# Rounded operands and rests in stick-breaking scores and values, and the HGRN2 output's last k tiles as two units

## The chip, the cores and the metric

The kernel runs on one core of a Trainium2 chip. The metric is the time of one execution on the device in microseconds; the median of several runs is compared. One profiled execution gives the trace.

## What is computed

A two-layer block (FoX attention, conv FFN, HGRN2, conv FFN) is followed by a hybrid block (retention and stick-breaking attention side by side, merged by gates, then SwiGLU). There are 512 tokens and 16 meta tokens, a width of 1024, all in fp32. The parts that the change touches are, in short:

```python
# HGRN2 mixer, after the heads
o = rms_norm(o, o_gain).reshape(B, L, D) * sigmoid(g)
h = h + o @ w_out
h = h + conv_ffn(h, ...)

# stick-breaking, 16 heads of 64
z = einsum('bhtd,bhsd->bhts', q, k) * scale
valid = (s_pos < t_pos) & (s_pos >= PAD)
log_not = where(valid, log_sigmoid(-z), 0)
after = cumsum(log_not, reverse over s) - log_not
a = where(valid, exp(log_sigmoid(z) + after), 0)
y = einsum('bhts,bhse->bhte', a, v)
```

## The kernel before

Everything is held transposed, features on the 128 partitions and the 528 tokens along them, so a width of 1024 is 8 tiles (`KT`). Weight products are made of rounded operands and rests: `wh`, `xh` are the fp32 values rounded to the type fp32r, `wl`, `xl` are what is left, and three fp32r matmuls (`wh` by `xh`, `wh` by `xl`, `wl` by `xh`) stand for one fp32 product. Such a product covers 528 tokens as two matmuls of 264 columns (L445), or 512 tokens as one (L441, a "narrow" group).

A *unit* is the weights for one output tile, up to 8 k tiles of 128x128. SyncE loads units into 4 slots of `raw` (`sp_unit`); ScalarE makes `wh` (`act_hi`, L404), VectorE makes `wl` (`dve_lo`, L408), each into 2 slots, one unit ahead of TensorE (`split_ahead`). A *group* is the accumulation of one output tile in PSUM (`pe_group`). Every engine runs its own list in order, and semaphores tie the lists together: `w_split`, `mm_done`, `psum_free`. `Phase` holds the numbers of units and groups of a stage, and the order of work on each engine is written out by hand.

**HGRN2 output.** The first 6 of 8 k tiles of the output product (`HG_EARLY`) are done during the last head. The last 2 k tiles are the phase `PH_HGOUT`: 8 groups, one for each output tile, of 12 matmuls each, each with a unit of its own (2 k tiles, 128 KB). For each tile VectorE adds the group to `h` (L516), ScalarE makes the gained copy `xh` (L463) and a square (L471), VectorE makes the rest `xl` (L475), and GpSimd adds the squares up (L486). Then the up-projection `PH_UP1` of the FFN follows.

**Stick-breaking.** The heads go two by two, with the loop of `sb_pair` on each engine. For a head TensorE makes the scores in PSUM from `s_k` and `s_q` (`sb_z`, L1034, fp32, 64 partitions), adds a mask (L1038), and after softplus it subtracts sums over later keys in fp32r (`sb_sums`, L1045, from the rounded `s_sh` and the rest `s_sl`). ScalarE turns the result into weights `s_a`, and `sb_values` (L1066, fp32) multiplies them by the transposed values `s_vt`; each head writes its own 64 partitions of PSUM bank 3. Softplus is Abs, Exp and Ln on ScalarE (L1540, L1543, L1546), a max-and-add on VectorE (L2249), a rounded copy on ScalarE and a rest on VectorE (L2253). Each of these works in three pieces, of 512, 400 and 432 columns.

Between these parts TensorE makes the four projections of the next pair (`ahead_`), in the order value, gate, query, key:

```python
            ahead_(0)
            if not isinstance(i, int) or i:
                sb_values(i - 1, 1)
            sb_sums(2 * i)
            ahead_(1)
            pe.wait_ge(s("sb_a"), 2 * i + 1)
            sb_z(1)
            ahead_(2)
            ...
            sb_values(i, 0)
            sb_sums(2 * i + 1)
            ahead_(3)
            ...
                sb_z(0)
```

`sb_turn` transposes the values of the next pair ahead of the last `sb_z(0)`.

## Time and profile before

| | |
|---|---|
| Median of 3 runs | 2936.13 us (2931.22 to 2941.09) |
| Profiled execution, its own time | 2934.11 us |
| Its span | 2932.4 us |
| TensorE (PE) busy | 2839.7 us, 97% |
| VectorE (DVE), ScalarE (ACT), GpSimd (POOL) busy | 1501.4, 1120.2, 210.7 us |
| Mean granted clock of TensorE | 0.985 |

PE is TensorE's matmuls, PEld its weight loads. Times in rows are microseconds from the start of the span. A fp32 matmul shows as two records in the trace, an fp32r matmul as one. Busy times of matmuls that follow each other overlap, so the time from start to start tells what one costs. A granted clock of 1.00 is 2.4 GHz, 0.50 is 1.2 GHz. An arrow `<-` names what ended the idle time before an instruction.

### The profile page before, as it was taken

The numbers are of one execution on the slowest core, as the hardware profiler recorded it, in microseconds if no ns is written. First come the engines' busy times: TensorE is split into PE (matmuls) and PEld (weight loads), VectorE is DVE, ScalarE is ACT, GpSimd is POOL, SyncE is SP. The second block draws the span as 40 slices with busy tenths as digits, with TensorE's granted clock in tenths as the row PEclk, the third lists the DMA queues.
The fourth block names the chain that finished last, engine by engine and source line by source line (L and its number), as shares of the span: only waits on it lengthen the run. The fifth ranks groups of instructions, "written<-read, shape, count | busy, mean of one in ns | idle before, by whom it ended". The sixth has DMA issues, their size and how long they took to land.

```text
span 2932.4 us, 46554 instructions
## 1 busy us (share of the span) xinstructions
PE 2839.7 (97%) x17851; PEld 2501.2 (85%) x17851; DVE 1501.4 (51%) x2168; ACT 1120.2 (38%) x1795; POOL 210.7 (7%) x177
## 2 busy tenths in 40 slices
PE   7999899999989999799999999999999999799998
PEld 7889799999989999799888888787888778588886
DVE  6767755553367775555533355364433335544422
ACT  4444443332245553433322223223344453422232
POOL 1000010000122220100001001001000000200000
PEclk9999999999999999899999999999999999899999
DMA  4222122323321111233233232332211112233322
GB/s 122 63 72 72 44 87 86 93 85 93 88 88 54 50 49 39 85 93 93 83 99 102 71 97 64 89 89 58 81 49 50 50 43 87 64 93 94 96 87 75
DMA packets 419559, 225.63 MB, mean 77 GB/s; under 512 B 7589, under 2 KB 416422, under 8 KB 419350
## 3 DMA queue, kind: packets, MB, share of 16 engines
q1 hardware_dynamic: 416438, 211.45, 24.9%
q0 software_dynamic: 2256, 10.32, 1.1%
q10 hardware_dynamic: 784, 2.75, 0.3%
q8 instruction: 55, 0.90, 0.1%
q14 instruction: 26, 0.21, 0.0%
HBM read 222.36 MB, written 2.13 MB: 77 GB/s over the span
## 4 chain that ended last, share of the span: by engine, by line
PE 63%; DVE 5%; issue 2%; ACT 1%; POOL 0%; DVEq 0%; ACTq 0%; POOLq 0%
PE ps L441 34%; PE ps L445 17%; PE ps L1045 2%; PE ps L861 2%; PE ps L1003 1%; PE ps L1066 1%; PE ps L1034 1%; PE ps L970 1%; DVE wl L408 1%; PE ps L906 1%; PE ps L1038 0%; DVE h L526 0%; DVE rl L2188 0%; DVE xl L475 0%; PE ps L895 0%
## 5 line engine op out<-in xcount | busy, mean ns | idle before, releaser
L408 DVE TENSOR_TENSOR wl<-raw,wh 128x1024 fp32r<-128x1024 f32 (+4 forms) x429 | 518.5, 1209 | 400.5 <-ACT wh L404 397.0
L404 ACT ACTIVATE wh<-raw 128x1024 fp32r<-128x1024 f32 (+4 forms) x429 | 428.4, 999 | 729.2 <-PE ps L441 395.1
L445 PE MATMUL ps<-xh,wh 128*128 128x264 f32 x2736 | 569.7, 289 | 13.4 <-DVE xl L475 6.0
L445 PE MATMUL ps<-xl,wh 128*128 128x264 f32 x2736 | 557.9, 285 | 0.0
L445 PE MATMUL ps<-xh,wl 128*128 128x264 f32 x2736 | 557.5, 285 | 0.0
L445 PEld LDWEIGHTS ps<-xh,wh 128*128 128x128 f32 x2736 | 428.4, 189 | 24.1 <-issue 6.1
L445 PEld LDWEIGHTS ps<-xl,wh 128*128 128x128 f32 x2736 | 425.6, 189 | 0.0
L445 PEld LDWEIGHTS ps<-xh,wl 128*128 128x128 f32 x2736 | 424.4, 189 | 0.0
L441 PE MATMUL ps<-xh,wh 128*128 128x512 f32 x976 | 392.2, 402 | 17.9 <-DVE xl L475 14.1
L441 PE MATMUL ps<-xl,wh 128*128 128x512 f32 x976 | 388.5, 398 | 0.0
L441 PE MATMUL ps<-xh,wl 128*128 128x512 f32 x976 | 386.1, 396 | 0.0
L441 PEld LDWEIGHTS ps<-xh,wh 128*128 128x128 f32 x976 | 184.5, 189 | 67.1 <-DVE xl L475 13.4
L441 PEld LDWEIGHTS ps<-xh,wl 128*128 128x128 f32 x976 | 185.2, 190 | 42.2
L441 PEld LDWEIGHTS ps<-xl,wh 128*128 128x128 f32 x976 | 184.7, 189 | 41.4 <-issue 1.4
L441 PE MATMUL ps<-hidh,wh 128*128 128x512 f32 x352 | 138.8, 394 | 0.4 <-DVE wl L408 0.4
L441 PE MATMUL ps<-hidh,wl 128*128 128x512 f32 x352 | 138.9, 395 | 0.0
L441 PE MATMUL ps<-hidl,wh 128*128 128x512 f32 x352 | 138.1, 392 | 0.0
L1729 DVE TENSOR_TENSOR pre<-ps,rstd 128x528 f32<-128x528 f32 (+1 forms) x66 | 46.4, 702 | 168.7 <-PE ps L445 110.4
L1729 DVE TENSOR_TENSOR t<-ps,rstd 128x512 f32<-128x512 f32 (+1 forms) x66 | 46.0, 697 | 145.7 <-PE ps L441 103.9
L486 POOL TENSOR_TENSOR ssq<-ssq,sq 128x528 f32<-128x528 f32 (+1 forms) x56 | 81.9, 1462 | 394.8 <-ACT sq L471 290.2
L1729 DVE TENSOR_TENSOR rt<-ps,rstd 128x512 f32<-128x512 f32 (+1 forms) x53 | 36.9, 697 | 141.7 <-PE ps L441 101.9
L488 POOL COPY ssq<-sq 128x528 f32<-128x528 f32 (+1 forms) x8 | 6.6, 826 | 1389.2 <-ACT sq L471 1130.5
(319 smaller groups left out, 4039.5 us busy)
## 6 DMA issues: line engine op xcount, KB each, us to landing
raw<-in_w_in SPq DMA_DIRECT2D x88, 512.0 KB, 4.0
raw<-in_ffn_w_gate SPq DMA_DIRECT2D x44, 512.0 KB, 3.8
raw<-in_ffn_w_up SPq DMA_DIRECT2D x44, 512.0 KB, 3.9
raw<-in_w_ffn_in SPq DMA_DIRECT2D x44, 512.0 KB, 3.8
raw<-in_fox_w_in SPq DMA_DIRECT2D x33, 512.0 KB, 4.1
raw<-in_hgrn_w_in SPq DMA_DIRECT2D x32, 512.0 KB, 4.0
raw<-in_ffn_w_down SPq DMA_DIRECT2D x32, 448.0 KB, 3.4
raw<-in_ffn_w_down SPq DMA_DIRECT2D x16, 512.0 KB, 3.6
```

Of the source, the lines that this page charges most:

```text
L404: nc.scalar.activation(wh[:, v % 2, 0:nk, :], raw[:, v % RAW_SLOTS, 0:nk, :], ACT.Copy).then_inc(s("w_hi"), 1)
L408: nc.vector.tensor_tensor(wl[:, v % 2, 0:nk, :], raw[:, v % RAW_SLOTS, 0:nk, :], wh[:, v % 2, 0:nk, :].bitcast(F32), ALU.subtract).then_in ...
L441: last = nc.tensor.matmul(ps[:, bank, 0:SEQ], w[:, slot, kk, :], x[:, k0 + k, META:L], start=first, stop=end_)
L445: last = nc.tensor.matmul(ps[:, bank + b, 0:HALF], w[:, slot, kk, :], x[:, k0 + k, b * HALF:(b + 1) * HALF], start=first, stop=end_)
L486: nc.gpsimd.tensor_tensor(ssq[:, t0:L], ssq[:, t0:L], sq[:, m % 2, t0:L], ALU.add).then_inc(s("sq_used"), 1)
L861: last = nc.tensor.matmul(ps[:, 2 + k % 2, P * c:P * (c + 1)], left[:, P * c:P * (c + 1)], right[:, P * c:P * (c + 1)], start=True, stop=True)
L906: last = nc.tensor.matmul(flat[:, at:at + TOK[j]], g_left[:, j * (j - 1) // 2 + c, :], g_f[:, P * j:P * j + TOK[j]], start=True, stop=True)
L970: last = nc.tensor.matmul(flat[0:TOK[j], at:at + SEQ - QFIRST[j]], rt[:, 2 + c, P * j:P * j + TOK[j]], rt[:, c, META + QFIRST[j]:L], start ...
L1003: last = nc.tensor.matmul(ps[:, 4 + e, QFIRST[j]:SEQ], r_vt[0:k, j, P * e:P * (e + 1)], r_s[0:k, QSTRIP[j]:QSTRIP[j] + SEQ - QFIRST[j]], s ...
L1034: nc.tensor.matmul(flat[:, QSTRIP[j]:QSTRIP[j] + SEQ - QFIRST[j]], s_k[lo:hi, P * j:P * j + P], s_q[lo:hi, QFIRST[j]:SEQ], start=(j < 3), ...
L1045: return nc.tensor.matmul(dst, w[:, :], src, start=False, stop=last, skip_group_check=True)
L1729: return V.tensor_tensor(shown(ph, gj, dst), out_of(ph, gj), shown(ph, gj, rstd[:, :]), ALU.mult)\
```

## The change

In stick-breaking, keys and queries are rounded (`sb_hi`, ScalarE) and their rests made (`sb_lo`, VectorE). `s_kp` holds for each head of the pair the rounded keys on its own 64 partitions and the rests on the other 64; `s_qh` and `s_ql` hold the rounded queries and their rests on both halves. A head's scores are two fp32r matmuls per key tile. The attention weights and the values are split the same way (`s_sh`, `s_sl`, `s_vh`, `s_vl`), and the values product is three fp32r matmuls per key tile. In `s_vh` and `s_vl` a block of zeros lies between the two heads' values, and both heads accumulate in all 128 partitions of bank 3. The order of the projections becomes key, query, value, gate. The buffers `s_sp`, `s_a` and `s_vt` go; their work moves to `s_e`, `s_sh` and `s_sl`. The outputs and gates lose their 16 meta columns.

At the HGRN2 output the last two k tiles become two units, each holding all 8 output tiles of one k tile (512 KB, rows that lie together), which are split before the last head's norm. TensorE still works output tile by output tile. ScalarE's squares run three tiles behind its copies, and VectorE's rests one tile behind its adds.

```diff
@@ phases
-PH_HGOUT = Phase(PH_HGL, 2, [[KT - HG_EARLY]] * 4, (0, 2) if ... else (2, 0))
+PH_HGOUT = Phase(PH_HGL, 1, [[KT]] * (KT - HG_EARLY), (0, 2) if ... else (2, 0))
+PH_HGOUT.gpi = KT
-PH_SB = Phase(PH_SBP, FOX_H // 2 - 1, K8, SB_BANKS, narrow=(1, 2))
+PH_SB = Phase(PH_SBP, FOX_H // 2 - 1, K8, SB_BANKS, narrow=(1, 3))
@@ SyncE: units of weights
+        for uj in range(PH_HGOUT.upi):
+            k = HG_EARLY + uj
+            sp_unit(sp, PH_HGOUT, 0, uj, dram["hgrn_w_out"][0][P * k:P * (k + 1), :].rearrange("p (m n) -> p m n", n=P))
...
-            sp_unit(sp, PH_SB, i, 0, sb_v(i, P))
-            sp_unit(sp, PH_SB, i, 1, gate_b(i, 0))
-            sp_unit(sp, PH_SB, i, 2, sb_q(i, P))
-            sp_unit(sp, PH_SB, i, 3, sb_k(i, P))
+            sp_unit(sp, PH_SB, i, 0, sb_k(i, P))
+            sp_unit(sp, PH_SB, i, 1, sb_q(i, P))
+            sp_unit(sp, PH_SB, i, 2, sb_v(i, P))
+            sp_unit(sp, PH_SB, i, 3, gate_b(i, 0))
@@ TensorE: HGRN2 output
+        for m in range(KT):
+            bank = PH_HGOUT.banks[(PH_HGOUT.g0 + m) % 2]
+            pe.wait_ge(s("psum_free"), PH_HGOUT.g0 + m + 1)
+            for uj in range(PH_HGOUT.upi):
+                k, slot = HG_EARLY + uj, (PH_HGOUT.u0 + uj) % 2
+                if m == 0:
+                    pe.wait_ge(s("w_split"), unit(PH_HGOUT, 0, uj) + RAW_SLOTS + 1)
+                    pe.wait_ge(s("y_ready"), KT + k + 1)
+                for n, (w, y) in enumerate(((wh, yh), (wh, yl), (wl, yh))):
+                    for b in range(2):
+                        last = nc.tensor.matmul(ps[:, bank + b, 0:HALF], w[:, slot, m, :], y[:, k, b * HALF:(b + 1) * HALF],
+                                                start=(uj + n == 0), stop=(uj + 1 == PH_HGOUT.upi and n == 2))
+                if m == KT - 1:
+                    last.then_inc(s("mm_done"), 1)
+            if m < KT - 1:
+                last.then_inc(s("late_mm"), 1)
@@ TensorE: scores and values
-                nc.tensor.matmul(flat[:, QSTRIP[j]:QSTRIP[j] + SEQ - QFIRST[j]], s_k[lo:hi, P * j:P * j + P],
-                                 s_q[lo:hi, QFIRST[j]:SEQ], start=(j < 3), stop=False, skip_group_check=True)
+                for n, q in enumerate((s_qh[:, b, :], s_ql[b][:, :])):
+                    nc.tensor.matmul(flat[:, QSTRIP[j]:QSTRIP[j] + SEQ - QFIRST[j]], s_kp[:, b, P * j:P * j + P],
+                                     q[:, QFIRST[j]:SEQ], start=(j < 3 and n == 0), stop=False, skip_group_check=True)
...
+            for ready, a, vs in (("sb_sh", s_sh, (s_vh, s_vl)), ("sb_sl", s_sl, (s_vh,))):
+                pe.wait_ge(s(ready), 6 * (2 * i + b) + 6)
+                for j in range(NTT):
+                    for v in vs:
+                        last = nc.tensor.matmul(ps[:, 3, QFIRST[j]:SEQ], v[:, j, b:b + 2, :].rearrange("p b n -> p (b n)"),
+                                                a[:, QSTRIP[j]:QSTRIP[j] + SEQ - QFIRST[j]], ...)
@@ TensorE: a pair
-            ahead_(0)
             if not isinstance(i, int) or i:
                 sb_values(i - 1, 1)
+            ahead_(0)
             sb_sums(2 * i)
             ahead_(1)
-            pe.wait_ge(s("sb_a"), 2 * i + 1)
+            pe.wait_ge(s("sb_a"), 6 * i + 3)
+            pe.wait_ge(s("sb_lo"), 2 * i + 2)
             sb_z(1)
-            ahead_(2)
-            pe.wait_ge(s("sb_vt_ready"), i + 1)
+            pe.wait_ge(s("sb_vt_lo"), i + 1)
             pe.wait_ge(s("sb_o_done"), i + 1)
             sb_values(i, 0)
+            ahead_(2)
             sb_sums(2 * i + 1)
             ahead_(3)
             if not last:
-                pe.wait_ge(s("psum_free"), evacuated(PH_SB, i, 0))
+                pe.wait_ge(s("psum_free"), evacuated(PH_SB, i, 2))
                 sb_turn()
-                pe.wait_ge(s("psum_free"), evacuated(PH_SB, i, 3))
-                pe.wait_ge(s("sb_a"), 2 * i + 2)
+                pe.wait_ge(s("sb_lo"), 2 * i + 3)
+                pe.wait_ge(s("sb_a"), 6 * i + 6)
                 sb_z(0)
@@ ScalarE
+            split_ahead(act, act_hi, PH_HGOUT, 0, 0)
             hgrn_rsqrt(i)
             hgrn_hi(i)
...
-        residual(PH_HGOUT, 3, ROW_FFN + KT)
+        for m in range(KT):
+            if m == KT - 1:
+                split_ahead(act, act_hi, PH_HGOUT, 0, 1)
+            act.wait_ge(s("psum_free"), evacuated(PH_HGOUT, 0, m))
+            copy(xh[:, m, :], h[:, m, :], scale=col(gains, m + ROW_FFN + KT)).then_inc(s("xh_ready"), 1)
+            if m >= 3:
+                act_square(act, 3, m - 3, m - 3, h[:, m - 3, :])
+        for m in range(KT - 3, KT):
+            act_square(act, 3, m, m, h[:, m, :])
...
+        def sb_hi(n, group, reads):
+            act.wait_ge(s("psum_free"), evacuated(*group))
+            for b in range(2):
+                if reads:
+                    act.wait_ge(s("sb_z"), 2 * n - 1 + b)
+                own_ = slice(FOX_D * b, FOX_D * (b + 1))
+                copy(s_kp[own_, b, 0:L], s_k[own_, :])
+                for half in (slice(0, FOX_D), slice(FOX_D, P)):
+                    last = copy(s_qh[half, b, :], s_q[own_, :])
+                last.then_inc(s("sb_hi"), 1)
...
                 act.wait_ge(s("sb_z"), n + 1)
+                if not isinstance(n, int) or n:
+                    act.wait_ge(s("sb_sl"), 6 * n)
...
+                if not isinstance(n, int) or n:
+                    act.wait_ge(s("sb_o_mm"), n)
                 for k, (c0, c1) in enumerate(QBANKS):
                     act.wait_ge(s("sb_sp"), 3 * n + k + 1)
-                    copy(s_sh[:, c0:c1], s_sp[:, c0:c1]).then_inc(s("sb_sh"), 1)
+                    copy(s_sh[:, c0:c1], s_e[:, c0:c1]).then_inc(s("sb_sh"), 1)
             def weights(n):
                 act.wait_ge(s("sb_acc"), n + 1)
                 for c0, c1 in QBANKS:
-                    last_ = nc.scalar.activation(s_a[:, c0:c1], flat[:, c0:c1], ACT.Exp)
-                last_.then_inc(s("sb_a"), 1)
+                    nc.scalar.activation(s_e[:, c0:c1], flat[:, c0:c1], ACT.Exp).then_inc(s("sb_a"), 1)
+                for k, (c0, c1) in enumerate(QBANKS):
+                    act.wait_ge(s("sb_a"), 3 * n + k + 1)
+                    copy(s_sh[:, c0:c1], s_e[:, c0:c1]).then_inc(s("sb_sh"), 1)
...
             split(2)
+            if not last:
+                sb_hi(i + 1, (PH_SB, i, 1), True)
             weights(2 * i + 1)
             split(3)
@@ VectorE
-        residual(PH_HGOUT, 3, ROW_FFN + KT)
+        for m in range(KT):
+            if m < KT - 1:
+                dve.wait_ge(s("late_mm"), m + 1)
+            else:
+                dve.wait_ge(s("mm_done"), group_end(PH_HGOUT, 0, PH_HGOUT.upi - 1))
+            V.tensor_tensor(two(h[:, m, :]), two(h[:, m, :]), out_of(PH_HGOUT, m), ALU.add).then_inc(s("psum_free"), 1)
+            if m:
+                dve_x(dve, 3, m - 1, ROW_FFN + KT)
+        split_ahead(dve, dve_lo, PH_HGOUT, 0, 1)
+        dve_x(dve, 3, KT - 1, ROW_FFN + KT)
...
+        def sb_lo(n):
+            for b in range(2):
+                own_, other = (slice(FOX_D * c, FOX_D * (c + 1)) for c in (b, 1 - b))
+                dve.wait_ge(s("sb_hi"), 2 * n + b + 1)
+                V.tensor_tensor(s_kp[other, b, 0:L], s_k[own_, :], s_kp[own_, b, 0:L].bitcast(F32), ALU.subtract)
+                for half in (own_, other):
+                    last = V.tensor_tensor(s_ql[b][half, :], s_q[own_, :], s_qh[own_, b, :].bitcast(F32), ALU.subtract)
+                last.then_inc(s("sb_lo"), 1)
...
+            dve.wait_ge(s("sb_vt_ready"), i + 1)
+            V.tensor_tensor(s_vl[:, 0:NFULL, 0:3:2, :], ps[:, 5, :].rearrange(...), s_vh[:, 0:NFULL, 0:3:2, :].bitcast(F32), ALU.subtract)
...
+            weights_lo(2 * i)
             split(1)
...
+                sb_query(PH_SB, i, 1)
             softplus(2 * i + 1)
             split(2)
...
+                scaled_out(PH_SB, i, 2, s_v[:, :])
+                sb_lo(i + 1)
+            weights_lo(2 * i + 1)
             split(3)
```

## Rows read from the trace of the kernel before

**Rows 1.** The page, parts 1 and 5: busy time; groups of instructions with mean ns

```profile
PE 2839.7 (97%) x17851; PEld 2501.2 (85%) x17851; DVE 1501.4 (51%) x2168; ACT 1120.2 (38%) x1795; POOL 210.7 (7%) x177
...
L408 DVE TENSOR_TENSOR wl<-raw,wh 128x1024 fp32r<-128x1024 f32 (+4 forms) x429 | 518.5, 1209 | 400.5 <-ACT wh L404 397.0
L404 ACT ACTIVATE wh<-raw 128x1024 fp32r<-128x1024 f32 (+4 forms) x429 | 428.4, 999 | 729.2 <-PE ps L441 395.1
...
L445 PEld LDWEIGHTS ps<-xh,wh 128*128 128x128 f32 x2736 | 428.4, 189 | 24.1 <-issue 6.1
```

**Rows 2.** Chain that ended last, one pair of stick-breaking: start us, us, what

```profile
2256.18 0.72 DVE s_k L1729
...
2257.02 2.62 PE ps L1034 x10
2259.64 0.65 PE ps L1038 x5
2260.29 5.95 PE ps L445 x48
2266.24 2.59 PE ps L1066 x10
2268.83 3.75 PE ps L1045 x26
```

**Rows 3.** The same chain at the HGRN2 output

```profile
1182.98 2.99 PE ps L445 x12
...
1199.64 0.70 DVE h L516
...
1201.52 0.77 DVE xl L475
```

**Rows 4.** Busy time by window, HGRN2 output: each engine (instructions), granted clock, DMA share, GB/s

```profile
1177.53:1208.64 31.11, 18.79 (x90) 17.02 (x91) 19.97 (x23) 12.31 (x21) 9.62 (x7) 0.69 0.28 81
```

**Rows 5.** Timeline of TensorE in one pair: start us, busy us, what, idle before

```profile
2247.06 0.77 PE L1045 MATMUL ps<-s_sl,tri_r 128*128 128x512 f32 x3
2247.66 1.28 PE L1045 MATMUL ps<-s_sh,one_r 128*128 128x400 f32 x10
2248.80 1.37 PE L1045 MATMUL ps<-s_sl,one_r 128*128 128x400 f32 x10
...
2257.02 2.62 PE L1034 MATMUL ps<-lnt,s_k 64*128 64x512 f32 x10 [0.33 <-DVE s_k L1729]
```

**Rows 6.** What writes the tile k_p: count, ns min/median/max, first and last start

```profile
L1145 ACT ACTIVATE k_p<-k_s x32: 639/644/646, 58.5 to 340.2; 64x528 fp32r<-64x528 f32 x32
```

**Rows 7.** Timeline of ScalarE in one pair; its scores ended at 2216.97

```profile
2217.03 1.42 ACT L1540 ACTIVATE s_e<-ps 128x512 f32<-128x512 f32 x3 [7.76 <-PE ps L1038]
...
2221.40 1.51 ACT L1145 ACTIVATE s_sh<-s_sp 128x512 fp32r<-128x512 f32 x3
```

**Rows 8.** Timeline of VectorE, ahead of the stage and in the same pair

```profile
2069.45 0.15 DVE L2223 MEMSET s_k<- 128x112 f32 x1
...
2222.09 1.69 DVE L2253 TENSOR_TENSOR s_sl<-s_sp,s_sh 128x512 fp32r<-128x512 f32 x3
```

**Rows 9.** Busy time by window, one pair: PE, PEld, DVE, ACT, POOL, clock

```profile
2212.80:2256.10 43.30, 42.97 (x254) 35.10 (x253) 14.79 (x21) 19.73 (x37) 0.00 (x0) 1.00 0.17 49
```

**Rows 10.** Timeline of GpSimd at the HGRN2 output

```profile
1201.98 1.47 POOL L486 TENSOR_TENSOR ssq<-ssq,sq 128x528 f32<-128x528 f32 x1 [2.54 <-ACT sq L471]
```

**Rows 11.** Busy time by window around changes of the granted clock

```profile
829.50:831.00 1.50, 0.08 (x1) 0.09 (x2) 1.50 (x3) 1.29 (x4) 1.50 (x2) 0.50 0.00 0
...
834.00:835.50 1.50, 1.50 (x10) 1.35 (x9) 1.50 (x2) 1.50 (x6) 1.50 (x2) 0.65 0.00 0
1176.50:1177.25 0.75, 0.00 (x0) 0.00 (x0) 0.48 (x1) 0.43 (x2) 0.00 (x0) 0.50 0.00 0
...
1186.25:1187.00 0.75, 0.00 (x0) 0.01 (x1) 0.75 (x2) 0.00 (x0) 0.34 (x1) 0.75 0.00 0
...
1592.00:1595.40 3.40, 3.39 (x10) 2.68 (x11) 0.80 (x2) 0.00 (x0) 0.00 (x0) 0.62 0.96 362
```

More of the change, by code:

```diff
@@ L298, in program @@
     assert b.at <= norms_at + 4 * L
-    gb = a.take("gb", [P, KT, L])
-    ga = a.take("ga", [P, 3, L])
-    oh = a.take("oh", [P, KT, L], F32R)
-    ol = a.take("ol", [P, KT, L], F32R)
+    b = Area(norms_at + 4 * 4 * L, arena)
+    s_qh, s_ql0 = b.take("s_qh", [P, 2, SEQ], F32R), b.take("s_ql0", [P, SEQ], F32R)
+    gb = a.take("gb", [P, KT, SEQ])
+    ga = a.take("ga", [P, 3, SEQ])
+    oh = a.take("oh", [P, KT, SEQ], F32R)
+    ol = a.take("ol", [P, KT, SEQ], F32R)
     s_q, s_v = lnt[:, META:L], sq[:, 0, :]
-    s_k = a.take("s_k", [P, NTT * P])
-    s_vt = a.take("s_vt", [P, NTT, P])
+    s_k = a.take("s_k", [P, L])
+    s_kp = a.take("s_kp", [P, 2, NTT * P], F32R)
+    s_ql = s_ql0, a.take("s_ql1", [P, SEQ], F32R)
+    s_vh, s_vl = (a.take(n, [P, NTT, 3, FOX_D], F32R) for n in ("s_vh", "s_vl"))
     s_e = a.take("s_e", [P, N_QSTRIP])
-    s_sp = a.take("s_sp", [P, N_QSTRIP])
     s_sh = a.take("s_sh", [P, N_QSTRIP], F32R)
     s_sl = a.take("s_sl", [P, N_QSTRIP], F32R)
-    s_a = a.take("s_a", [P, N_QSTRIP])
     m_t = post_t
@@ L440, in pe_group @@
                     if gj in ph.narrow:
-                        last = nc.tensor.matmul(ps[:, bank, 0:SEQ], w[:, slot, kk, :], x[:, k0 + k, META:L],
-                                                start=first, stop=end_)
+                        last = nc.tensor.matmul(ps[:, bank, 0:SEQ], w[:, slot, kk, :],
+                                                x[:, k0 + k, x.shape[2] - SEQ:x.shape[2]], start=first, stop=end_)
                         continue
@@ L958, in _ @@
         hgrn(HG_H - 1, True)
-        for i in range(2):
-            for gj in range(4):
-                pe_group(pe, PH_HGOUT, i, gj, yh, yl, ("y_ready", KT + HG_EARLY) if i + gj == 0 else None, HG_EARLY)
+        for m in range(KT):
[14 more added lines that the diff above has]
+                last.then_inc(s("late_mm"), 1)
         feed_forward(1, PH_UP1, PH_DOWN1, 3, 3)
@@ L1061, in sb_values @@
         def sb_values(i, b):
-            lo, hi = FOX_D * b, FOX_D * (b + 1)
-            pe.wait_ge(s("sb_a"), 2 * i + b + 1)
-            for j in range(NTT):
-                k = TOK[j]
-                last = nc.tensor.matmul(ps[lo:hi, 3, QFIRST[j]:SEQ], s_vt[0:k, j, lo:hi],
-                                        s_a[0:k, QSTRIP[j]:QSTRIP[j] + SEQ - QFIRST[j]], start=(j == 0), stop=(j == NFULL))
+            for ready, a, vs in (("sb_sh", s_sh, (s_vh, s_vl)), ("sb_sl", s_sl, (s_vh,))):
[3 more added lines that the diff above has]
+                        last = nc.tensor.matmul(ps[:, 3, QFIRST[j]:SEQ], v[:, j, b:b + 2, :].rearrange("p b n -> p (b n)"),
+                                                a[:, QSTRIP[j]:QSTRIP[j] + SEQ - QFIRST[j]],
+                                                start=(b == 0 and a is s_sh and v is s_vh and j == 0),
+                                                stop=(b == 1 and a is s_sl and j == NFULL))
             last.then_inc(s("sb_o_mm"), 1)
@@ L1521, in _ @@
         tables_for(act, "ln_exp")
[L1522 to L1525 removed]
+        copy(ident_r[:, :], ident)
+        copy(later_r[:, :], neg_tri, scale=1e30)
+        copy(tri_r[:, :], neg_tri)
+        copy(one_r[:, :], neg_one)
         plain(PH_SBP)
+        def sb_hi(n, group, reads):
[8 more added lines that the diff above has]
+                last.then_inc(s("sb_hi"), 1)
+        sb_hi(0, (PH_SBP, 0, 1), False)
         def sb_out(i):
@@ L1530, in sb_out @@
             carry(act, "act_carry")
-            copy(row(oh, i)[:, META:L], ps[:, 3, :]).then_inc(s("sb_o_hi"), 1)
+            copy(row(oh, i), ps[:, 3, :]).then_inc(s("sb_o_hi"), 1)
         def sb_pair(i, last=False):
@@ L2221, in _ @@
             V.tensor_tensor(yr[:, m, META:L], yr[:, m, META:L], rt[:, m, META:L], ALU.mult)
-        own(V.memset(s_k[:, L:NTT * P], 0.0))
+        own(V.memset(s_kp[:, :, L:NTT * P].bitcast(F32), 0.0))
+        for v in (s_vh, s_vl):
+            own(V.memset(v[:, :, 1, :].bitcast(F32), 0.0))
+            own(V.memset(v[:, NFULL, 0:3:2, :].bitcast(F32), 0.0))
         def sb_query(ph, i, gj):
```

85 lines of the change are left out of this document (45 added, 40 removed).

## The prediction

> **What bounds the kernel.** I read the page first. TensorE is busy for 97% of the span, and nothing else is near it [rows 1]. So a change pays only where it shortens TensorE's own work or fills one of its gaps. The edit has two sites, and I read the chain of waits at each.
>
> In the stick-breaking stage (2086.2 to 2431.4) the chain is TensorE's own work, pair after pair, 43.30 us each; per head it holds 2.56 to 2.62 us of fp32 scores (L1034) and 2.59 us of fp32 values (L1066). The one other member is the store of `s_k`, 0.72 us per pair [rows 2].
>
> At the HGRN2 output (1177.53 to 1208.64) the chain leaves TensorE: 12 matmuls, then add to `h`, a gained copy, a rest, a weight split, then 12 matmuls [rows 3]. Of these 31.11 us TensorE is busy 18.79, at a mean granted clock of 0.69 [rows 4].
>
> **Scores.** Before, a head runs 5 fp32 products over 512+400+272+144+16 = 1344 columns. After, it runs 10 fp32r products, twice 1344 columns: the rounded keys and their rests lie in the two halves of the partitions, so one product takes both. Price of fp32r here [rows 5]: 512+400+432 columns take 2247.66-2247.06 = 0.60 us, and ten products of 400, 2x272, 3x144, 4x16 columns take 1.14. With 0.235 for 512, 0.19 for 400 and 0.13 for 272, the seven narrow ones are left with 0.69, or 0.10 each. The nearest other row, 5 products of at most 128 columns in 0.65 (L1038 in [rows 2]), gives 0.13. One pass over the 1344 columns is thus 0.235+0.19+0.13+2x0.10 = 0.755, at most 0.815. Two passes, with a little at the switch: 1.55 (bounds 1.45 to 1.63). Before: 2.58. A head saves 1.03.
>
> **Values.** 5 fp32 products become 15 fp32r ones: hi by hi, lo by hi, hi by lo; both heads add into one bank, the other head's 64 weight columns being zero. Three passes: 2.30 (2.20 to 2.45), against 2.59. A head saves 0.29. Sixteen heads: 16 x 1.32 = 21.1 us (17.4 to 25).
>
> A page rule looks at this otherwise. The Trainium skill, "FP8 and Floating Point Precision", TensorE Precision Notes, counts true FP32 as four passes through the array; this trace records each fp32 product as two, so it doesn't settle the count. If its passes cost alike, the new products do 2/4 and 3/4 of the work of the old: scores 1.29, values 1.94, and the sum would be 10 us better than mine.
>
> **The wait for keys.** Before, the last projection of a pair is the key, and the next scores wait for its store: TensorE is idle 0.33 us behind its transposes [rows 5]. After, key and query come first and gate last, so this goes for seven pairs: 2.3 us. What is late next is worked out below.
>
> **What the other engines get, per pair.** ScalarE: 6 copies for keys and queries on 64 partitions, priced by the FoX copies of the same kind, 0.64 each [rows 6], and 2x3 copies of the weights at 1.51 per three [rows 7]: 6.8 us. VectorE: 6 rests at 0.70, as its other passes over 528 columns [rows 3], 2x3 rests at 1.69 [rows 8], two for the values (0.9): 8.5 us. They have 19.73 and 14.79 of 43.30 busy [rows 9]; 26.5 and 23.3 of about 40 are no bound. Only order can hurt, so I walk a pair, with 0 where its first scores end and TensorE running free: values of the last head to 2.3; key projection 8.3; sums 12.0; query 17.7; scores 19.9; values 22.2; v 28.1; sums 31.9; gate 37.6; transposes 38.2; scores 40.4.
> - Sums at 8.3 need the rests of softplus. Abs starts at +0.06, the copy of sums begins 4.4 later [rows 7], and the last rest ends 6.8 after the scores [rows 8]. Cover 1.5, and the second sums the same. The new wait in front of these copies (for the values before, done at 2.3) is over by then. The new wait in front of Abs (weight rests of the last head) was over at about -5.
> - The second scores need `sb_lo`, stored a pair earlier; the transposes' V rests: ScalarE's copies wait for `sb_out`, which VectorE reaches after the key store at 9.0, so they are there at 11.6, against 19.9.
> - `sb_hi` stands behind a weight split and ahead of the exps on ScalarE: 26.8 to 30.2, exps free at 31.9. `sb_lo` on VectorE starts after the v store at 28.9 and ends near 33, ahead of the weight rests (35.2) and the last split (37). The next scores ask at 38.2: cover 5; the next values at 40.4: cover 5.
> - If a cover is gone, that much of every pair is lost. Queued behind `sb_lo` are the weight rests, split and gate store, so a late `sb_lo` holds all of TensorE's next pair.
>
> SP issues the same four transfers of a pair in another order. Five memsets replace one (0.15, [rows 8]) ahead of a split with little cover: +0.2 once. Stage: -21.1-2.3+0.2 = -23.2.
>
> **HGRN2 output.** The same 96 matmuls, but k tile by k tile: 2 units of 512 KB in place of 8 of 128 KB, the same bytes, 6 issues fewer on SP. Both are split before the last head's norm; the second adds about 0.15 us to its chain (the copy ends at 1172.95, where the Ln could start at 1172.8). The first 6 matmuls run early, as before. The other 90 start at 1177.7, and no split stands between tiles. VectorE's period per tile is 0.70+0.77 [rows 3], GpSimd's 1.47 [rows 10], under TensorE's 12 x 0.125 = 1.5 at full clock.
>
> The clock: it is at half by 1176.5, while TensorE waits for the last head's norm, and rises at 1186.6, 9 us after the restart, in which there were idle gaps. Elsewhere work came back at 831 and went on without a gap, and the clock rose at 835, 4 later [rows 11]. I take 5.5, between 4 and 9. At half clock 12 matmuls take 2.99 with the start and the end of the burst [rows 3]; in a run of them I take 264 columns at 1.2 GHz, 0.22 each (25 in 5.5 us). At full clock a projection of 48 takes 5.95 [rows 2], so 65 x 0.125 = 8.1. End 1191.3 (1190.6 to 1192.9). Then up-projection 1 waits for its first split. ScalarE, behind the copy of tile 6 and the square of tile 3, makes `wh` (1.0, [rows 1]) at +0.75 to +1.8; VectorE `wl` (1.2, [rows 1]) to +3.1; TensorE starts at +3.2 = 1194.5. Such a gap can cost clock: after 3.0 idle us up to 1592.0 it fell for a while (0.62 in the mean over 3.4 us [rows 11]), so 3.4 x 0.38/0.5 = 2.6 us at half, 1.3 of work lost; as it need not happen, I put in 0.9. GpSimd's adds lag by three tiles: the four left after ScalarE's square at +3.0 end near +9.0, and the first projection group at 3.2+6.0 = 9.2. Cover 0.2. So 1195.4 instead of 1208.64: -13.3 (-9 to -16).
>
> **Sum.** -23.2-13.3 = -36.5. The profiled execution took 2934.11 (span 2932.4), giving 2897.6; the median shown is 2.0 above it, giving 2899.6. I say 2899.
>
> **Rivals.**
> - A, forecast: 2899, own range 2888 to 2910. Chance 0.62.
> - B, one site gives little. The HGRN2 output stays at half clock to its end and into the up-projection, or the sum for the norm comes late (cover 0.2): -6 instead of -13, 2907. Or in the stick-breaking stage a rest arrives late at a wait; 1.5 us per pair is 12, 2911. For it: the thin covers of 0.2 and 1.5; against: the engines' load. Chance 0.25.
> - C, an fp32r product costs a quarter of an fp32 one whatever its width: scores 2/4 of 2.58 = 1.29, values 3/4 = 1.94, together 16 x 1.94 = 31 saved instead of 21: 2889. (This is what the four passes of the Trainium skill's "FP8 and Floating Point Precision" would give.) Against it: the fp32r rows, where narrow products stay at 0.10 and don't shrink with columns. Chance 0.08.
> - D, slower: weight loads not hidden. Each new product has weights of its own; if each paid a load (0.19, [rows 1]) besides its columns, scores would take 10x0.19+1.12 = 3.0 and values 15x0.19+1.68 = 4.5, +2.35 per head, +37.6; less 2.3 and 13.3: +22, 2958. It decides from about 0.11 unhidden per product on (25 x 16 x 0.11 = 44). Against it: the starts in [rows 5], 0.1 apart. Chance 0.03. That the change leaves the time alone (the gains of both sites eaten by waits): 0.02.
>
> A difference of 0.3%, about 9 us, is what a measurement of this kernel can tell from none. A and C, and nearly all of B, are beyond it: faster 0.94, same 0.03, slower 0.03. Range 2886 to 2914: it takes in C and B's price, and leaves out some 0.15.
>
> **What the profile after would show.** Scores 1.55 and values 2.3 per head in the chain; 40.2 us per pair; no store of `s_k` in it; ScalarE near 26, VectorE near 23 per pair; 16 to 18 us from 1177.7 to the first up-projection, with full clock from about 1183. I'd be wrong if TensorE waits for `sb_lo`, `s_sl` or `s_vl` in every pair, if narrow fp32r products with new weights cost over 0.13, or if the clock stays at half beyond 1187.

## The result, and the profile after

The changed kernel takes 2892.34 us (median of 4 runs, 2891.34 to 2892.86), against 2934.31 for the kernel before on the same chip: a ratio of 0.9853, 95% interval 0.9838 to 0.9869. The forecast was 2899, range 2886 to 2914; as a difference it was 36.5 us, and 42.0 were measured. The profiled execution took 2892.77, with a span of 2891.1.

Line numbers moved. In the profile after, scores are L1051 (L1034 before), the mask L1055, sums L1062, values L1084, the transposes L1118, a wide projection L449, a narrow one L445, the HGRN2 output L974, the add to `h` L2179, a rest `xl` L479, a split `wl` L412, GpSimd's adds L490.

The page's first part, busy times ([rows 1] before):

```profile
PE 2808.8 (97%) x17931; PEld 2511.4 (87%) x17931; DVE 1568.0 (54%) x2278; ACT 1169.6 (40%) x1885; POOL 212.4 (7%) x177
```

TensorE still bounds the kernel, with 30.9 us less of work. Next the chain that ended last, for one pair of the stick-breaking stage (start us, us, what), to be held against [rows 2]:

```profile
2151.33 0.55 PE ps L1118 x5
2151.87 1.42 PE ps L1051 x10
2153.29 0.56 PE ps L1055 x5
2153.85 2.29 PE ps L1084 x15
2156.14 6.00 PE ps L449 x48
2162.14 3.56 PE ps L1062 x26
2165.70 5.66 PE ps L445 x24
...
2191.36 1.43 PE ps L1051 x10
```

From scores to scores a pair takes 2191.36-2151.87 = 39.49 us, against 43.30 [rows 9]. No member is a store or a wait: `s_k` is gone from the chain, and nothing took its place. The pair's window (columns as in [rows 9]) shows the load of the other engines:

```profile
2151.90:2191.40 39.50, 39.50 (x262) 36.66 (x262) 23.32 (x36) 26.13 (x49) 0.00 (x0) 1.00 0.18 53
```

VectorE 23.3 and ScalarE 26.1, as worked out in the forecast, and TensorE busy for all of it.

The same chain at the HGRN2 output ([rows 3] before):

```profile
1176.68 11.03 PE ps L974 x66
...
1188.43 1.81 DVE xl L479
1190.25 0.61 DVE h L2179
1190.86 1.12 DVE xl L479
1191.98 0.63 DVE h L2179
1192.61 2.74 issue
1195.35 8.09 PE ps L449 x48
...
1209.88 5.85 PE ps L449 x48
```

The reader is to see three things. TensorE starts at 1176.68 and reaches the first up-projection at 1195.35: 18.67 us instead of the 31.11 of [rows 4]. The chain leaves TensorE at 1187.7 for VectorE, whose rests take 1.81 and 1.12 in it, where one took 0.77 [rows 3]. And the first up-projection takes 8.09, where a group of its kind takes 6.0.

Where the 41.3 us between the two spans (2932.4 and 2891.1) lie, by positions in the two traces:

| place | before | after | shift so far |
|---|---|---|---|
| wait for an early store of `h`, ahead of the output | 1158.56 | 1157.52 | -1.04 |
| second up-projection group | 1221.18 | 1209.88 | -11.30 |
| first scores | 2086.20 | 2074.72 | -11.48 |
| end of the last values | 2431.38 | 2389.77 | -41.61 |

So the output gives 10.3, the stick-breaking stage 30.1 (345.18 to 315.05), and 1 us is drift of stages that neither edit touches.

### The profile page after: what moved, and what is told of

It is laid out like the page before. It is cut to its first block, busy times and chain, and to the rows that moved or that the text cites. A ratio compares the mean times of both kernels' runs of the same rounds, so it can differ in the third digit from the quotient of the medians.

```text
span 2891.1 us, 46967 instructions
## 1 busy us (share of the span) xinstructions
PE 2808.8 (97%) x17931; PEld 2511.4 (87%) x17931; DVE 1568.0 (54%) x2278; ACT 1169.6 (40%) x1885; POOL 212.4 (7%) x177
## 4 chain that ended last, share of the span: by engine, by line
PE 89%; DVE 6%; issue 2%; ACT 1%; POOL 1%; DMA 0%; DVEq 0%; ACTq 0%; POOLq 0%
PE ps L449 39%; PE ps L445 34%; PE ps L1062 2%; PE ps L866 2%; PE ps L1021 1%; PE ps L1084 1%; PE ps L689 1%; PE ps L784 1%; PE ps L1051 1%; PE ps L988 1%; DVE wl L412 1%; PE ps L770 1%; PE ps L911 1%; POOL ssq L490 1%; PE ps L772 1%
## 5 line engine op out<-in xcount | busy, mean ns | idle before, releaser
L408 ACT ACTIVATE wh<-raw 128x1024 fp32r<-128x1024 f32 (+3 forms) x423 | 425.9, 1007 | 732.6 <-PE ps L445 395.1
L412 DVE TENSOR_TENSOR wl<-raw,wh 128x1024 fp32r<-128x1024 f32 (+3 forms) x423 | 511.3, 1209 | 322.7 <-ACT wh L408 316.8
L449 PE MATMUL ps<-xh,wh 128*128 128x264 f32 x2736 | 570.6, 290 | 15.9 <-DVE xl L479 5.4
L449 PE MATMUL ps<-xh,wl 128*128 128x264 f32 x2736 | 558.4, 286 | 0.0
L449 PE MATMUL ps<-xl,wh 128*128 128x264 f32 x2736 | 558.4, 286 | 0.0
L449 PEld LDWEIGHTS ps<-xh,wh 128*128 128x128 f32 x2736 | 429.1, 189 | 27.3 <-issue 9.5
L449 PEld LDWEIGHTS ps<-xl,wh 128*128 128x128 f32 x2736 | 426.2, 189 | 0.0
L449 PEld LDWEIGHTS ps<-xh,wl 128*128 128x128 f32 x2736 | 425.2, 189 | 0.0
L445 PE MATMUL ps<-xh,wh 128*128 128x512 f32 x976 | 392.1, 402 | 17.6 <-DVE xl L479 13.8
L445 PE MATMUL ps<-xl,wh 128*128 128x512 f32 x976 | 388.3, 398 | 0.0
L445 PE MATMUL ps<-xh,wl 128*128 128x512 f32 x976 | 386.5, 396 | 0.0
L445 PEld LDWEIGHTS ps<-xh,wh 128*128 128x128 f32 x976 | 184.5, 189 | 67.2 <-DVE xl L479 13.8
L445 PEld LDWEIGHTS ps<-xh,wl 128*128 128x128 f32 x976 | 185.1, 190 | 41.8
L445 PEld LDWEIGHTS ps<-xl,wh 128*128 128x128 f32 x976 | 184.8, 189 | 41.5 <-issue 1.4
L445 PE MATMUL ps<-hidh,wh 128*128 128x512 f32 x352 | 138.8, 394 | 0.4 <-DVE wl L412 0.4
L445 PE MATMUL ps<-hidh,wl 128*128 128x512 f32 x352 | 138.9, 395 | 0.0
L445 PE MATMUL ps<-hidl,wh 128*128 128x512 f32 x352 | 138.1, 392 | 0.0
L490 POOL TENSOR_TENSOR ssq<-ssq,sq 128x528 f32<-128x528 f32 (+1 forms) x56 | 83.3, 1488 | 375.3 <-ACT sq L475 270.2
```

The lines of the kernel that those rows point to most:

```text
L408: nc.scalar.activation(wh[:, v % 2, 0:nk, :], raw[:, v % RAW_SLOTS, 0:nk, :], ACT.Copy).then_inc(s("w_hi"), 1)
L412: nc.vector.tensor_tensor(wl[:, v % 2, 0:nk, :], raw[:, v % RAW_SLOTS, 0:nk, :], wh[:, v % 2, 0:nk, :].bitcast(F32), ALU.subtract).then_in ...
L445: last = nc.tensor.matmul(ps[:, bank, 0:SEQ], w[:, slot, kk, :], x[:, k0 + k, x.shape[2] - SEQ:x.shape[2]], start=first, stop=end_)
L449: last = nc.tensor.matmul(ps[:, bank + b, 0:HALF], w[:, slot, kk, :], x[:, k0 + k, b * HALF:(b + 1) * HALF], start=first, stop=end_)
L490: nc.gpsimd.tensor_tensor(ssq[:, t0:L], ssq[:, t0:L], sq[:, m % 2, t0:L], ALU.add).then_inc(s("sq_used"), 1)
```

## The experiments

All compare with the kernel before on the same chip. Its medians were 2934.45 (e1 to e4), 2932.52 (e5 to e8) and 2934.92 (e9 to e11). "Above the changed kernel" is against its 2892.34, another set of runs. The changed kernel was 42.0 us below the kernel before in its own set and 43.3 in that of e11, so a difference of 1 or 2 us between sets tells nothing.

**Output alone (e1_output_alone).** The kernel before with only the hunks of the HGRN2 output.

> Only the HGRN2 output is changed, the stick-breaking stage is that of before. If the two parts add up, the traces put 11.3 us to this one (second up-projection group at 1209.9 instead of 1221.2): 2923 where before is 2934, ratio 0.996. Rival, that the parts help each other: less than 8 us here. The first up-projection group should again start some 18.7 us after the first matmul behind the norm, and run 8.1 us.

Measured: 2923.45 us (2921.19 to 2926.00), ratio 0.9957 (0.9941 to 0.9974), so -11.0. The two sites add up: 11.0 here, and 31 is left for stick-breaking. The chain of this kernel shows the same slow rest and the same slow first group:

```profile
1188.56 1.81 DVE xl L477
...
1195.46 8.07 PE ps L447 x48
```

**Values as before (e2_values_fp32).** From the changed kernel; the rests are still made, and the product leaves them out.

```diff
-            for ready, a, vs in (("sb_sh", s_sh, (s_vh, s_vl)), ("sb_sl", s_sl, (s_vh,))):
...
+                last = nc.tensor.matmul(ps[FOX_D * b:FOX_D * (b + 1), 3, QFIRST[j]:SEQ], s_vh[0:k, j, 2 * b, :].bitcast(F32),
+                                        s_sh[0:k, QSTRIP[j]:QSTRIP[j] + SEQ - QFIRST[j]].bitcast(F32), ...)
```

> The changed kernel, but the values are one fp32 product of the rounded operands (the rests are made and not used). Values should take 2.6 us per head instead of 2.30: +4.7 us over 16 heads. Two theories for why the sums went from 3.75 to 3.55: (switch) an fp32r product behind an fp32 one pays about 0.2, then the projection that now stands behind the fp32 values grows from 6.0 to 6.2 and the whole by 3 us more; (narrow end) the next weight load is bare behind a product of 16 columns, whatever its type, then that projection stays at 6.0 and the sums, behind a wide projection, at 3.55.

Measured: 2898.28 us (2896.54 to 2899.56), ratio 0.9874 (0.9858 to 0.9891): 5.9 above the changed kernel. Of its chain:

```profile
2173.56 2.59 PE ps L1084 x10
2176.15 6.05 PE ps L449 x48
2182.20 3.55 PE ps L1062 x26
```

Values cost 2.59 as fp32 and 2.29 to 2.30 as fp32r: 0.29 per head, as in the forecast; the projection behind them adds 0.05 to 0.09. The sums stay at 3.55 behind a wide projection. Of the two theories in the expectation this speaks against the first: a projection behind an fp32 product would have taken 6.2.

**Scores as before (e3_scores_fp32).** From the changed kernel; the rests of keys and queries are made and left out of the product.

```diff
-                for n, q in enumerate((s_qh[:, b, :], s_ql[b][:, :])):
-                    nc.tensor.matmul(flat[...], s_kp[:, b, P * j:P * j + P], q[:, QFIRST[j]:SEQ], ...)
+                nc.tensor.matmul(flat[...], s_kp[own_, b, P * j:P * j + P].bitcast(F32), s_qh[own_, b, QFIRST[j]:SEQ].bitcast(F32), ...)
```

> The changed kernel, but the scores are one fp32 product of the rounded operands on 64 partitions (the rests are made and not used). Scores should take 2.58 instead of 1.42: +18.6 us. Switch theory: the mask behind them goes back from 0.56 to 0.65 (+1.5 us). Narrow end: it stays at 0.56.

Measured: 2912.53 us (2910.82 to 2913.41), ratio 0.9922 (0.9906 to 0.9939): 20.2 above the changed kernel. Of its chain:

```profile
2176.85 2.56 PE ps L1051 x10
2179.40 0.65 PE ps L1055 x5
```

Per head 2.56+0.65 here against 1.43+0.56 after: 1.22, times 16 is 19.5 of the 20.2. The five mask products are the same work in both; they cost 0.09 more behind an fp32 product. That is what the first theory said, and the second had them stay at 0.56. So neither theory holds for both e2 and e3, and why a neighbour costs what it does stays open.

**A fourth term (e4_fourth_term).** Rest by rest added to the values: 5 more fp32r products per head, everything else alike.

```diff
-            for ready, a, vs in (("sb_sh", s_sh, (s_vh, s_vl)), ("sb_sl", s_sl, (s_vh,))):
+            for ready, a, vs in (("sb_sh", s_sh, (s_vh, s_vl)), ("sb_sl", s_sl, (s_vh, s_vl))):
```

> The changed kernel with the fourth term as well, rest of the weights by rest of the values: five more fp32r products per head. If TensorE alone bounds the stage, each head grows by one pass, 0.70 to 0.76 us: +11 to +12 us. If another engine or a wait bounds part of it, clearly less. If a pass cost a quarter of an fp32 product, 0.65: +10.3.

Measured: 2905.85 us (2904.81 to 2909.21), ratio 0.9899 (0.9882 to 0.9915): 13.5 above. Its chain has

```profile
2159.92 3.07 PE ps L1084 x20
```

against 2.29 for 15, so one pass costs 0.775 and 16 of them 12.4. It shows two things at once: that a pass isn't a quarter of an fp32 product (0.65), and that TensorE alone sets the pace of the stage, since work added to it comes through in full. In this execution the stage takes 12.4 us more than in the changed kernel's (its end is 16.2 later, its entrance 3.7). Of the 3.7, 3.5 were there when the 90 matmuls of the output began (1180.13), far ahead of the edit; the clock had fallen at 363 us and at 813. The window of this kernel at 363 has a granted clock of 0.72, where the changed kernel's shows 1.00:

```profile
363.00:369.00 6.00, 5.53 (x25) 3.14 (x26) 0.92 (x3) 0.42 (x3) 0.00 (x0) 0.72 0.01 3
```

**Without GpSimd's adds (e5_no_adds).** In the changed kernel, the seven adds of squares behind the HGRN2 output are left out, so the norm of the following FFN is not the reference's.

```diff
-                nc.gpsimd.tensor_tensor(ssq[:, t0:L], ssq[:, t0:L], sq[:, m % 2, t0:L], ALU.add).then_inc(s("sq_used"), 1)
+                if r == 3:
+                    pool.sem_inc(s("sq_used"), 1)
+                else:
...
```

> The changed kernel without GpSimd's seven adds of squares at the HGRN2 output (only the first square is copied, so the norm ahead of the second FFN is wrong). Theory: VectorE's rests of 1.9, 1.2 and 1.6 us at the end of the output are 0.76 us ones that wait for, or share with, GpSimd's adds. Then all rests take 0.76 here and the gap ahead of the up-projection shrinks from 4.7 to about 3.2 us. Rival, that the rests are slow for another reason (ScalarE's copy late): the durations stay. The clock falls in the gap either way if idle time is what matters; if it stays up the first group takes 6.1 instead of 8.1.

Measured: 2890.21 us, a single run, which settles nothing by its time. The trace does: the chain no longer leaves TensorE within the 90 matmuls:

```profile
1175.56 13.68 PE ps L977 x90
...
1192.10 8.73 PE ps L449 x48
```

All rests take 0.76 to 0.77, the gap ahead of the up-projection is 2.9 us instead of 4.7, and from the first of the 90 matmuls to the up-projection it takes 16.54 instead of 18.67. The first group is still slow (8.73): the gap that is left costs the clock all the same.

**The two gaps filled (e6_filled_gaps).** 30 matmuls into a free bank while the last head's norm is computed, 32 between the output and the up-projection; their results are overwritten.

```diff
+                    if uj:
+                        pe.wait_ge(s("psum_free"), PH_HGOUT.g0 + 2)
+                        for n in range(30):
+                            nc.tensor.matmul(ps[:, PH_HGOUT.banks[...], 0:HALF], wh[...], yh[:, HG_EARLY, 0:HALF], start=True, stop=True)
...
+        for n in range(32):
+            nc.tensor.matmul(ps[:, 4, 0:HALF], yh[:, HG_EARLY, 0:P], yh[:, HG_EARLY, 0:HALF], start=True, stop=True)
         feed_forward(1, PH_UP1, PH_DOWN1, 3, 3)
```

> The changed kernel with matmuls whose result nobody reads in TensorE's two gaps: 30 while it waits for the last head's norm, 32 ahead of the up-projection. Theory: the clock stays at 1.00 through both, so the output's first 28 matmuls take 0.125 instead of 0.22 (-2.7 us) and the first up-projection group 6.1 instead of 8.1 (-2.0 us), together 4 to 5 us less than the changed kernel. Rival: with the clock up, VectorE and GpSimd pace the output (1.5 us per tile), so the first part comes back as idle time and only 2 us stay.

Measured: 2889.39 us (2886.95 to 2892.59), ratio 0.9851 (0.9835 to 0.9868). Its chain:

```profile
1176.17 3.87 PE ps L974 x30
1180.04 11.01 PE ps L979 x90
...
1195.80 6.09 PE ps L449 x48
```

And its window over the same stretch, where the 1.00 is the granted clock:

```profile
1180.00:1215.00 35.00, 34.12 (x251) 32.31 (x250) 24.92 (x28) 20.62 (x28) 11.83 (x8) 1.00 0.20 57
```

The clock stays at 2.4 GHz. The 90 matmuls take 11.01 us instead of 13.9, and the first group 6.09 instead of 8.09. From the last early projection group (the 36 matmuls ahead of the last head's norm) to the end of the first up-projection group it takes 32.8 instead of 37.2 us, 4.4 less. The time doesn't show it: e6 is 43.1 us below the kernel before of its set, the changed kernel 42.0 in its own, and the intervals of the two ratios overlap. In this execution the clock also fell at 363 and 813 (0.72 in both windows, as in e4), and the last early group began at 1169.13, 2.9 us later than in the changed kernel.

**VectorE's split first (e7_split_first).** The split for the up-projection goes ahead of the rest of tile 6, and ScalarE's squares are no longer three tiles late.

```diff
-            if m >= 3:
-                act_square(act, 3, m - 3, m - 3, h[:, m - 3, :])
+            if m < KT - 2:
+                act_square(act, 3, m, m, h[:, m, :])
...
+            if m == KT - 1:
+                split_ahead(dve, dve_lo, PH_HGOUT, 0, 1)
             if m:
                 dve_x(dve, 3, m - 1, ROW_FFN + KT)
-        split_ahead(dve, dve_lo, PH_HGOUT, 0, 1)
```

> The changed kernel with squares right behind the copies (not three tiles late) and, at the last tile, both halves of the weight split ahead of the square and the rest. Theory: TensorE's gap ahead of the up-projection goes from 4.7 to about 3 us, since one rest and the contention with GpSimd leave the path; 1.5 us less than the changed kernel, 3.5 if the clock also stays up. Rival: the adds of GpSimd now lie beside every tile's rest and slow the tiles down, so that the gap's gain is lost before it.

Measured: 2892.61 us (2889.50 to 2895.59), ratio 0.9866 (0.9850 to 0.9883): no gain in the median, where 1.5 had been expected. With the squares early, GpSimd adds beside every tile, and all of VectorE's rests but the first take 1.2 to 1.5. That eats most of what the split gains, as the rival in the expectation said: 17.9 us from the first of the 90 to the up-projection, against 18.7.

**Slower rests in stick-breaking (e8_slow_rests).** Behind each head's `sb_lo`, three more subtractions on VectorE, 0.66 each, hold up the semaphore; they read the queries and write a spare buffer.

```diff
+                for c in range(3):
...
+                    V.tensor_tensor(dummy[:, :], s_q[:, 0:472], s_q[:, 0:472], ALU.subtract).then_inc(s("dummy"), 1)
```

> The changed kernel with three more subtractions of 472 columns on VectorE for each head in front of the signal that the rests of keys and queries are ready, each waiting for the one before: about 4.4 us more VectorE work per pair. The trace shows 4.6 us between the last rest (2186.6) and the scores that need it (2191.2). Theory: all of it lies in that cover, 0 to 2 us in all. Rival, that the cover is thinner (weight rests, split and gate store queue behind it): up to 3 us per pair, 24 in all.

Measured: 2901.16 us (2897.57 to 2902.66), ratio 0.9889 (0.9872 to 0.9905): 9 above, outside the 0 to 2 of the theory and well below the 24 of the rival. Its window of a pair shows the old pace, with 3.5 us more of VectorE in it:

```profile
2140.99:2180.60 39.61, 39.61 (x263) 36.74 (x262) 26.86 (x41) 26.12 (x49) 0.00 (x0) 1.00 0.19 54
```

Its chain shows the loss at the entrance of the stage:

```profile
2083.69 0.72 DVE sq L1781
...
2084.45 1.33 PE ps L1119 x5
```

So the pairs don't notice: nearly 5 us more of VectorE per pair fit into their cover, about half of them ahead of the next scores. But ahead of the first pair the store of the values (`sq`, L1781) stands behind `sb_lo` on VectorE, and the transposes wait for it. In the changed kernel it ended at 2075.67, 0.9 us before the transposes began. Here TensorE waits 0.6 us ahead of the first scores and 3.3 ahead of the transposes, and the clock falls behind the wait (0.83 in the mean from 2085 to 2092): from the entrance to the end of the next projection it takes 5.6 us more. The other 3.5 us were there ahead of the edit, by 1180.15, when the 90 matmuls of the output start (1176.68 in the changed kernel); again the clock had fallen at 363 and 813.

**Both remedies, each alone in its order, and the changed kernel again (e9_both, e10_split_first_late_squares, e11_changed_again).** e10 puts VectorE's split ahead of the rest of tile 6, ScalarE's split ahead of the square of tile 3, and four squares, instead of three, behind the last copy; e9 does that and fills the gaps with 30 and 22 matmuls. All ran on one chip.

```diff
+                act_square(act, 3, m - 4, m - 4, h[:, m - 4, :])
...
-            if m >= 3:
+            if 3 <= m < KT - 2:
...
-        for m in range(KT - 3, KT):
+        for m in range(KT - 4, KT):
```

> The changed kernel with the fillers (30 while TensorE waits for the norm, now ahead of its wait for the second split, and 22 ahead of the up-projection) and with both halves of the first up-projection split ahead of the last but one tile's square and rest; the squares stay three tiles late. Theory: 4.7 us for the clock (2.7 at the output, 2.0 at the first group) and about 1.4 for one rest less on the path: 6 us less than the changed kernel, about 2886, if the sum for the norm isn't late. Rival: GpSimd's last add ends at a time that neither edit moves (1201.1 in the trace of the changed kernel), so that an earlier first group only waits for it: then the sum for the norm starts at about the same time and 2 to 3 us stay.

> The changed kernel with the split ahead of square 3 and rest 6, squares still three tiles late, no fillers. Theory: the gap ahead of the up-projection goes from 4.7 to about 3.3 us, the tiles before it keep their pace, and the first group still runs at half clock (8.1): 1 to 1.5 us less than the changed kernel.

> The changed kernel once more beside e9 on one chip: 2892, ratio 0.985.

| | us | ratio |
|---|---|---|
| e9_both | 2888.58 (2887.00 to 2889.66) | 0.9841 (0.9828 to 0.9855) |
| e10_split_first_late_squares | 2891.99 (2890.56 to 2894.94) | 0.9858 (0.9843 to 0.9873) |
| e11_changed_again | 2891.66 (2891.48 to 2892.08) | 0.9853 (0.9838 to 0.9868) |

e9 has the lowest ratio of the case. It is 3.1 us below the changed kernel on the same chip, and their ranges don't touch; the 2 to 3 of the rival, then, and not the 6 of the theory. For the order of work alone (e10) 1 to 1.5 us less were expected, and the medians show none. The traces show more. From the start of the last early projection group to the start of the second up-projection group it takes 43.6 us in the changed kernel (43.3 in e11), 42.4 in e7, 41.6 in e10, 39.6 in e9 and 39.5 in e6. So e10 does gain some 2 us there, e9 gains no more than e6 did by filling alone, and what comes between executions from elsewhere hides gains of this size. Why e9 doesn't gain 6, its chain shows:

```profile
1189.07 1.83 POOL ssq L490
...
1196.00 1.31 POOL ssq L490
...
1197.35 1.16 PE ps L500 x4
```

The up-projection no longer sets the end, the sum of squares does. GpSimd adds from 1189.07 to 1197.31 almost without a break, and the matmuls that finish the norm (L500) wait for it, 1.45 us in e9 and as much in e10. This is the place where the forecast had a cover of 0.2 us. In the changed kernel the adds ended at 1201.07 and these matmuls began at 1203.27: the late and slow first group had made it 2.2.

## Why the prediction was right

**Scores.** Forecast 1.55 (1.45 to 1.63), measured 1.42 to 1.43: just below the lower bound. A pass over 1344 columns in the scores costs 0.71, not 0.755. The term that was off is the price of a product, taken from sums in which every product has other weights and other columns. The changed kernel's TensorE timeline shows them one by one:

```profile
2171.20 0.40 PE L1051 MATMUL ps<-s_qh,s_kp 128*128 128x512 f32 x1
2171.43 0.39 PE L1051 MATMUL ps<-s_ql,s_kp 128*128 128x512 f32 x1
...
2172.35 0.28 PE L1051 MATMUL ps<-s_ql,s_kp 128*128 128x144 f32 x1
2172.46 0.22 PE L1051 MATMUL ps<-s_qh,s_kp 128*128 128x16 f32 x1
2172.53 0.26 PE L1051 MATMUL ps<-s_ql,s_kp 128*128 128x16 f32 x1
2172.64 0.70 PE L1055 MATMUL ps<-later_r,ident_r 128*128 128x112 f32 x5
```

A product with another `s_kp` tile starts 0.11 behind the one ahead of it (2172.46), the second with the same tile 0.07 behind the first (2172.53): 0.09 in the mean, where 0.10 was put in. The six wide products take 1.08 by their starts, where the forecast's prices give 1.11; they were a little high, since with 0.235 for 512 columns and 0.19 for 400 the sum of 0.60 leaves 0.175 for 432. And nothing shows of the 0.04 put in for the switch. By the chain it is 0.125 a head, 2.0 us over 16 heads.

**Values.** 2.30 forecast, 2.29 to 2.30 measured.

**The neighbours.** This is what the forecast left out, and it makes most of the missing 7 us of the stage. Mask: 0.65 before, 0.56 after, over 16 heads 1.5 us; e3 gives it back with fp32 scores, so it is shown. Sums: 3.75 before [rows 2], 3.55 after, over 15 heads 3.0 us. They used to follow fp32 values and now follow a projection. The trace of the kernel before has the comparison itself, in the sums of the first head, which no values precede:

```profile
2090.03 5.87 PE ps L445 x48
2095.90 3.55 PE ps L1045 x26
```

In e2 the values are fp32 again and stand ahead of the projection, and the sums stay at 3.55, so their gain hangs on what stands directly in front of them. Whether sums directly behind fp32r values would cost 3.55 too was not tried.

**The wait for keys.** Forecast 0.33 a pair. Wait and transposes together took 0.86 before and take 0.55 after, 0.31: right. Of the 0.5 us that are left, 0.2 are the price of the memsets, which cost nothing (below); the others were not separated. The stage in all: -23.2-2.0-1.5-3.0-0.5 = -30.2, measured -30.1.

**Covers and loads.** ScalarE 26.1 and VectorE 23.3 against "near 26" and "near 23"; no wait in the pair. VectorE's `sb_lo` ends at 2186.6 for scores that start at 2191.4, 4.8 us, against the 5 of the walk. But these scores wait for the first head's rests only (the semaphore's value in the code is 2i+3), and those end at 2184.5: the cover is 6.9, larger than walk and expectation of e8 have it. e8 put 2.4 us on it and left 4.5. The thinnest cover of a pair, that of the sums, was walked as 1.5: the rests of softplus end at 2160.7 and 2180.3, the sums start at 2162.1 and 2181.6, so 1.4 and 1.3. It held. The five memsets were priced at 0.2 and cost nothing that shows: TensorE's wait there is 0.8 us, as before. What the walk didn't look at is the entrance of the stage, where the value store has a cover of 0.9 (e8). It held.

**HGRN2 output.** Forecast -13.3, measured -10.3: within its own range of -9 to -16. Three terms are off.

- The clock's half: 5.5 us taken, 6.1 measured. These are windows of TensorE (total, busy, granted clock, DMA share, GB/s):

```profile
1175.75:1176.50 0.75, 0.00 (x0) 0.62 0.89 266
1182.50:1183.25 0.75, 0.75 (x8) 0.83 0.00 0
1193.00:1193.75 0.75, 0.00 (x0) 0.50 0.00 0
```

It had fallen when the 90 matmuls began at 1176.68 and rose about 1182.8. The 90 took 13.9 us, to 1190.6, where 13.6 had been forecast.

- The gap behind them: 3.2 forecast, 4.7 measured. VectorE's period per tile was taken as 0.70+0.77, with GpSimd beside it at no cost. The two engines' timelines say otherwise, VectorE first:

```profile
1186.88 0.76 DVE L479 SCALAR_TENSOR_TENSOR xl<-h,gains,xh 128x528 fp32r<-128x528 f32 x1
...
1188.35 1.90 DVE L479 SCALAR_TENSOR_TENSOR xl<-h,gains,xh 128x528 fp32r<-128x528 f32 x1
...
1191.90 0.69 DVE L2179 TENSOR_TENSOR h<-h,ps 128x528 f32<-128x528 f32 x1
1192.52 1.59 DVE L479 SCALAR_TENSOR_TENSOR xl<-h,gains,xh 128x528 fp32r<-128x528 f32 x1
1194.03 1.21 DVE L412 TENSOR_TENSOR wl<-raw,wh 128x1024 fp32r<-128x1024 f32 x1
```

and GpSimd:

```profile
1188.35 1.33 POOL L490 TENSOR_TENSOR ssq<-ssq,sq 128x528 f32<-128x528 f32 x1 [0.23 <-ACT sq L475]
...
1192.24 1.31 POOL L490 TENSOR_TENSOR ssq<-ssq,sq 128x528 f32<-128x528 f32 x1 [0.82 <-ACT sq L475]
1194.35 2.07 POOL L490 TENSOR_TENSOR ssq<-ssq,sq 128x528 f32<-128x528 f32 x1 [0.80 <-ACT sq L475]
```

The rest that begins at 1188.35, at the same time as GpSimd's add, ends at 1190.25, 0.57 behind the end of the add (1189.68). The one at 1192.52 ends at 1194.11, 0.56 behind the add's end (1193.55). A rest thus ends as if it had waited for the add that is under way and then done its own work. The split at 1194.03 began first and isn't slowed (1.21); there GpSimd's add takes 2.07. The add to `h`, which reads one operand from PSUM, takes 0.69 or 0.70 throughout. Without the adds (e5) every rest takes 0.76 and the gap is 2.9, near the 3.2 of the forecast. So the term that failed is VectorE's period, and the cause is shown. The Trainium skill has the rule, "SBUF — State Buffer", Who interferes with whom: a VectorE instruction with two SBUF inputs and a GpSimd instruction that reads SBUF exclude each other, and the one that starts first runs through; with at most one SBUF input, and outside its 2-port modes, VectorE isn't touched. The trace agrees in all three points. The trace of before had a sign of it too: at 1185.36 a split of 128x256 took 1.51 us beside an add of GpSimd, where the same split took 0.42 at 1177.39.

- The clock in that gap: 0.9 was put in for a fall that might happen, which was thought to cost 1.3 if it does. That 1.3 was read from a window of [rows 11] that ends at 1595.4; in the same trace the matmuls of 512 columns stay 0.43 apart, instead of 0.23, until 1596.2, so that fall cost 1.6. Here it happened (0.50 at 1193, 0.95 in the slice from 1199.75 on), and the first up-projection took 8.09 instead of 6.09: 2.0. It fell again in e5, whose gap was 2.9. With the gap filled (e6) it did not fall.

Together: clock +0.3, gap +1.5, fall +1.1, and the norm's chain, 0.2 longer where 0.15 was put in, next to nothing; -13.3 becomes -10.3.

**Rivals.** A, the forecast, came true, but that the total is so near is partly luck: two misses of opposite sign, 7 us more from stick-breaking and 3 less from the output, and 1 us of drift. (Of the 6.7 us between 2899 and 2892.3, 1.8 are the kernel before itself, whose median over four runs is that much lower than the one that the forecast started from.) B (one site gives little) did not: output 11.0 alone (e1), stage 30.1. C, a quarter of an fp32 product whatever the width, would give 1.29 and 1.94 per head; it is refuted by values at 2.30 and by e4's 0.775 per pass. The scores alone wouldn't decide: 1.42 lies midway between its 1.29 and A's 1.55. The measured 2892 even lies nearer to its 2889 than to the 2899 of A: a time that fits is no proof of a mechanism. The count of four passes in the Trainium skill's "FP8 and Floating Point Precision" gives no price here: an fp32 product over these columns costs 2.59/0.775 = 3.3 passes of fp32r in the values and 2.58/0.71 = 3.6 in the scores. D, weight loads unhidden, fails by the starts 0.07 and 0.11 apart.
